# A two-layer hybrid decoder step on one core: feed-forwards that multiply the unnormed sum, low-rank products inside the r and k products, and the first scan unit prepared inside v

## The reference

```python
for i in range(DEPTH):                       # DEPTH = 2
    h = attention(x) if i == 0 else rwkv7_time_mix(x)
    x = layer_norm(ALPHA * x + h, ln_g[i, 0], ln_b[i, 0])
    gu = x @ w_gu[i]
    ffn = (silu(gu[..., :D_FF]) * gu[..., D_FF:]) @ w_down[i]
    x = layer_norm(ALPHA * x + ffn, ln_g[i, 1], ln_b[i, 1])
# rwkv7_time_mix: xr, xw, xk, xv, xa, xg = (x + xx * mix[c] for c in range(6)), xx = previous token - x
# r, k, v = xr @ w_r, xk @ w_k, xv @ w_v
# w = f(tanh(xw @ w1) @ w2), a = sigmoid(a0 + (xa @ a1) @ a2), g = sigmoid(xg @ g1) @ g2
# then a delta-rule scan over the tokens, a group norm, a gate by g and an output product
```

## Time and profile before

| | us |
|---|---|
| median of 3 runs | 1932.48 (1930.57 to 1932.52) |
| the profiled execution | 1942.81 |
| its span | 1941.0 |
| TensorE busy | 1706.0 |
| VectorE, ScalarE, GpSimd busy | 651.9, 687.3, 587.1 |

### The profile page before, as it was taken

The page is one execution under the profiler, slowest core; times in us unless marked ns, Lnnn a source line. Parts: engine busy times, 40 slices in busy tenths (PEclk is TensorE's granted clock), DMA queues, the critical chain, the costliest instruction groups (busy, mean ns, idle before and its releaser), DMA issues.

```text
span 1941.0 us, 46539 instructions
## 1 busy us (share of the span) xinstructions
PE 1706.0 (88%) x20338; PEld 1552.7 (80%) x20338; DVE 651.9 (34%) x897; ACT 687.3 (35%) x1110; POOL 587.1 (30%) x322
## 2 busy tenths in 40 slices
PE   4987969999989967898958888888797999998995
PEld 4975959999989967696647766666496999998995
DVE  2145562222223344404153444443165222222224
ACT  3146253333322122322254455443225333321113
POOL 2324423333333421232142222220142333333430
PEclk8998989999999986999978999999597999999998
DMA  8410222222223213321100001000221222222221
GB/s 249 88 41 1 76 74 87 86 76 86 83 74 89 74 36 102 103 72 48 35 4 15 15 15 26 16 10 10 93 75 43 77 86 76 86 81 84 74 74 49
DMA packets 236120, 125.88 MB, mean 65 GB/s; under 512 B 49211, under 2 KB 233068, under 8 KB 235828
## 3 DMA queue, kind: packets, MB, share of 16 engines
q1 hardware_dynamic: 230770, 113.53, 20.7%
q10 hardware_dynamic: 5218, 10.36, 1.5%
HBM read 116.33 MB, written 12.64 MB: 66 GB/s over the span
## 4 chain that ended last, share of the span: by engine, by line
PE 49%; issue 34%; POOL 7%; DVE 6%; ACT 3%; POOLq 0%; ACTq 0%; DVEq 0%
PE ps L699 32%; POOL wl L552 7%; PE ps L1013 1%; PE ps L904 1%; PE ps L1023 1%; PE ps L1103 1%; ACT S L1490 1%; DVE mf L2069 1%; PE ps L1093 1%; PE ps L1114 1%; PE ps L790 1%; PE ps L1144 1%; PE ps L937 1%; PE ps L1050 0%; PE ps L992 0%
## 5 line engine op out<-in xcount | busy, mean ns | idle before, releaser
L552 POOL TENSOR_TENSOR wl<-raw,wh 128x1024 fp32r<-128x1024 f32 (+1 forms) x172 | 453.5, 2638 | 891.3 <-ACT wh L1371 891.3
L699 PE MATMUL ps<-xh,wh 128*128 128x288 f32 x2112 | 462.4, 301 | 61.8 <-DVE xl L1868 21.0
L1371 ACT CAST wh<-raw 128x1024 fp32r<-128x1024 f32 (+1 forms) x172 | 190.3, 1108 | 829.4 <-PE ps L699 819.9
L699 PE MATMUL ps<-xl,wh 128*128 128x288 f32 x2112 | 457.8, 299 | 0.0
L699 PE MATMUL ps<-xh,wl 128*128 128x288 f32 x2112 | 457.4, 299 | 0.0
L699 PEld LDWEIGHTS ps<-xh,wh 128*128 128x128 f32 x2112 | 345.4, 192 | 73.3 <-issue 41.4
L699 PEld LDWEIGHTS ps<-xl,wh 128*128 128x128 f32 x2112 | 346.1, 192 | 0.0
L699 PEld LDWEIGHTS ps<-xh,wl 128*128 128x128 f32 x2112 | 345.8, 192 | 0.0
L1944 DVE TENSOR_TENSOR lnw<-lnw,ps 128x576 f32<-128x576 f32 x44 | 33.2, 755 | 390.4 <-PE ps L699 373.3
L699 PE MATMUL ps<-hh,wh 128*128 128x288 f32 x704 | 153.3, 300 | 11.3 <-DVE hl L1949 11.3
L699 PE MATMUL ps<-hl,wh 128*128 128x288 f32 x704 | 152.5, 299 | 0.0
(11 more groups left out here) (332 smaller groups left out, 2174.6 us busy)
## 6 DMA issues: line engine op xcount, KB each, us to landing
raw<-in_ffn_w_gu SPq DMA_DIRECT2D x88, 512.0 KB, 3.8
raw<-in_ffn_w_down SPq DMA_DIRECT2D x32, 704.0 KB, 4.5
raw<-in_rwkv_w_rkv SPq DMA_DIRECT2D x24, 512.0 KB, 3.6
raw<-in_attn_w_qkv SPq DMA_DIRECT2D x24, 256.0 KB, 3.7
raw<-in_attn_w_o SPq DMA_DIRECT2D x32, 128.0 KB, 2.9
raw<-in_rwkv_w_o SPq DMA_DIRECT2D x8, 512.0 KB, 3.6
spread<-table ACTq DMA_DIRECT2D x1, 3072.0 KB, 14.5
x_kept<-x SPq DMA_DIRECT2D x1, 2304.0 KB, 8.8
```

The source lines that it names most:

```text
L552: nc.gpsimd.tensor_tensor(wl[:, s, 0:ph.kb, :], raw[:, s, 0:ph.kb, :], wh[:, s, 0:ph.kb, :].bitcast(F32), ALU.subtract).then_inc(raw_free, 1)
L699: out = mm(ps[:, 2 * a + b, 0:TH], w[:, s, k, :], o[:, k0 + k, t0:t0 + TH], start=(first and k == 0 and w is wh and o is high), stop=(last ...
L1371: nc.scalar.copy(wh[:, s, 0:ph.kb, :], raw[:, s, 0:ph.kb, :]).then_inc(hi_done, 1)
```

## The change

Four things are changed.

1. **Feed-forwards.** After wo and ro, ScalarE multiplies each finished block of the sum by the norm's weight into the high part (`summed_product`), VectorE subtracts to get the low part (`add_and_pass_on`); no mean is taken off and nothing is scaled. The operand tiles get two more columns in their first half (`WIDE = TH + 2`, 290 of 288): the norm's weight and its bias, so that each up slab also gives the products of weight row and bias row with the weights. TensorE starts the first up slab on these; the first waits for the columns of blocks 0 to 5, and at block 6 for those of 6 and 7. The statistics' products stand after the first up slab. VectorE scales each output from PSUM by the inverse deviation and adds the two columns' parts (mean times the first, plus the second), for the gate before Silu and for the up part before the product: eight VectorE instructions per hidden block where there were two. The normed, ALPHA-scaled x that the residual needs is made in the loop, a block per round. The loops of ScalarE and VectorE over hidden blocks are written out.
2. **Down products** wait for each hidden block on its own.
3. **r, k, v.** The last slab of wo, r, k and ro counts each operand block that it has used (`given_up`), and the next operand's parts may overwrite that block. Decay and rate products stand between the blocks of r's slabs 2 to 5 (both for the same block, one to each column half), the gate products between the blocks of k's first slab, the shift rows' transposes before r's slab 6.
4. **Slot 0 of the scan** is taken out of the loop and done during v: TensorE's two small products before slab 4 and key sums before slab 6, ScalarE's steps after slabs 3, 5 and 7, GpSimd's between its splits; to have room, `hats` and the first `bt` use other tiles. SP loads the first states when v's operand is complete. The gate's second weights are loaded by ScalarE after v's last read-out; GpSimd's clears of the scan's tiles move with it.

The core of the diff:

```diff
 def slab(..., op=None, between=None, release=None, hidden=None, columns=None):       # TensorE
     for k in range(kb):
         if op is not None:
             pe.wait_ge(op_ready, KB * OP[op] + k + 1)
+        if columns is not None and k in (0, KB - 2):
+            pe.wait_ge(ev("ln_cols"), columns + (1 if k == 0 else 2))
+        if hidden is not None:
+            pe.wait_ge(hid_lo, hidden + k0 + k + 1)
         for w, o in ((wh, high), (wh, low_), (wl, high)):
             for b, t0 in halves:
-                out = mm(ps[:, 2 * a + b, 0:TH], w[:, s, k, :], o[:, k0 + k, t0:t0 + TH],
+                wide = high is sum_h
+                n = WIDE if wide and b == 0 else TH
+                out = mm(ps[:, 2 * a + b, 0:n], w[:, s, k, :],
+                         o[:, k, b, 0:n] if wide else o[:, k0 + k, t0:t0 + TH],
...
+        elif release is not None:
+            out.then_inc(release, 1)
+        if between is not None:
+            between(k)
...
-                pe.wait_ge(hid_lo, FB * (i_ffn + 1))
...
-            norm(0, PH["wo"])
             ffn(0)
...
+            def lora_wa(k):
+                if k == 0:
+                    pe.wait_ge(ev("lora_w_in"), 16 * 6)
+                pe.wait_ge(ev("mf"), 2 * k + 2)
+                for b, t0 in halves:
+                    for w, part, own in ((w1s, top, 0), (a1s, low, 1)):
+                        out = mm(ps[part, 4 + b, 0:TH], w[:, k, :], mf[:, own, t0:t0 + TH], start=(k == 0), stop=(k == KB - 1))
+                out.then_inc(ev("mf_used"), 1)
...
+            mixed_product("r", before={6: shift_rows}, between={m: lora_wa_in(m) for m in range(2, 6)}, release=ev("given_up"))
+            mixed_product("k", between={0: lora_g}, release=ev("given_up"))
+            mixed_product("v", before={4: lambda: lora2(0), 6: lambda: kk_sum(0)})
...
+            def summed_product(name, i_ln):                                          # ScalarE
...
+                def high(j):
+                    act.wait_ge(ev("given_up"), GIVEN[name] + min(j + 2, KB - 1))
+                    A(sum_h[:, j, :, 0:TH], x[:, j, :].rearrange("p (h n) -> p h n", h=2), ACT.Identity, scale=col(R_LNG + i_ln, j)
+                      ).then_inc(op_hi, 1)
...
+                high_ahead(ph, KB - 2, 0, True)
+                squares(KB - 2)
+                for j in range(KB - 2):
+                    high(j)
+                act.wait_ge(ev("given_up"), GIVEN[name] + KB - 1)
+                columns(0, KB - 2)
+                high_ahead(ph, KB - 1, 1, True)
...
+                        g, h = gbuf[:, q, :], hbuf[:, q, :]                            # VectorE, ffn
+                        V.tensor_copy(gate_sc[:, q, :], ps[:, 4 * q, TH:WIDE]).then_inc(ev("ffn_step"), 1)
+                        V.tensor_tensor(halved(g), acc(2 * q), halved(rsd), ALU.mult).then_inc(gate_free, 1)
+                        V.scalar_tensor_tensor(g, centre, gate_sc[:, q, 0:1], g, ALU.mult, ALU.add).then_inc(ev("ffn_step"), 1)
+                        V.tensor_copy(up_sc[:], ps[:, 4 * q + 2, TH:WIDE]).then_inc(ev("ffn_step"), 1)
+                        V.tensor_tensor(halved(h), acc(2 * q + 1), halved(rsd), ALU.mult).then_inc(ev("ffn_step"), 1)
+                        V.scalar_tensor_tensor(h, centre, up_sc[:, 0:1], h, ALU.mult, ALU.add).then_inc(ev("ffn_step"), 1)
+                        dve.wait_ge(ev("gated"), n + 1)
+                        V.scalar_tensor_tensor(h, h, up_sc[:, 1:2], g, ALU.add, ALU.mult).then_inc(up_free, 1)
+                        V.tensor_tensor(hl[:, 2 * i + q, :], h, hh[:, 2 * i + q, :].bitcast(F32), ALU.subtract).then_inc(hid_lo, 1)
...
+                    if i < KB:
+                        normed(i)
...
+                def low_part(j):                                                      # VectorE, add_and_pass_on
+                    dve.wait_ge(op_hi, op + j + 1)
+                    V.scalar_tensor_tensor(sum_l[:, j, :, 0:TH], x[:, j, :].rearrange("p (h n) -> p h n", h=2), col(R_LNG + i_ln, j),
+                                           sum_h[:, j, :, 0:TH].bitcast(F32), ALU.mult, ALU.subtract).then_inc(op_ready, 1)
...
+                added(ph, KB // 2 - 1, 0)
+                summed(ph, i_ln, KB // 2 - 1, 0)
+                for j in range(KB - 2):
+                    low_part(j)
+                columns(0, KB - 2, 1)
+                added(ph, KB // 2 - 1, 1)
+                low_part(KB - 2)
+                low_part(KB - 1)
+                columns(KB - 2, KB, 2)
+                summed(ph, i_ln, KB // 2 - 1, 1)
...
+                        dve.wait_ge(ev("given_up"), (KB - 1) * step + j + 1)           # VectorE, mix
...
-            sp.wait_ge(ev("proj_taken"), 1)
+            sp.wait_ge(op_ready, KB * (OP["v"] + 1))
             sp.wait_ge(ev("x_moved"), 16)
             state_in(0)
             state_in(1)
...
+            split_two(PH["v"], 1)                                                     # GpSimd
+            pool.wait_ge(op_ready, KB * (OP["v"] + 1))
+            nc.gpsimd.memset(cc_s[:], 0.0)
+            nc.gpsimd.memset(cc[:], 0.0).then_inc(ev("wkv_zero"), 1)
+            split_two(PH["v"], 2)
+            split_two(PH["v"], 3)
+            scaled_gate(0)
+            scaled_r(0)
+            scaled_keys(0)
...
-            for s in range(SLOTS):
+            for s in range(1, SLOTS):
```

More of the change, by code:

```diff
@@ L690, in _, with slab @@
             ident = const("ident")
-            def slab(a, s, kb, high, low_, k0, first, last, op=None):
+            def slab(a, s, kb, high, low_, k0, first, last, op=None, between=None, release=None, hidden=None, columns=None):
                 for k in range(kb):
@@ L711, in two_slabs @@
                         pe.wait_ge(acc_free, 2 * i + (ph.m0 + s + 1))
-                        slab(s, s, ph.kb, high, low_, 0, True, True, op)
+                        slab(s, s, ph.kb, high, low_, 0, True, True, op, release=release if s == 1 else None)
                 two_slabs(0, op)
-                with nc.tensor.Fori(1, ph.slabs // 2 - int(before_last is not None)) as i:
+                with nc.tensor.Fori(1, ph.slabs // 2 - int(apart)) as i:
                     two_slabs(i)
@@ L717, in product, with mixed_product @@
                     before_last()
-                    two_slabs(ph.slabs // 2 - 1)
+                if apart:
+                    two_slabs(ph.slabs // 2 - 1, release=release)
+            def mixed_product(name, before={}, between={}, release=None):
+                ph = PH[name]
+                for m in range(ph.slabs):
+                    if m in before:
+                        before[m]()
+                    pe.wait_ge(raw_free, m + ph.n0 + 3)
+                    pe.wait_ge(acc_free, m + ph.m0 + 1)
+                    slab(m % 2, m % 2, ph.kb, xh, xl, 0, True, True, name if m < 2 else None, between.get(m),
+                         release if m == ph.slabs - 1 else None)
             def cache_keys():
@@ L890, in _ @@
             pe.wait_ge(ev("o_taken"), U // 2)
-            product("wo", None)
-            norm(0, PH["wo"])
+            product("wo", None, release=ev("given_up"))
             ffn(0)
-            norm(1, PH["dn0"])
-            def lora_in(step, products):
-                for k in range(KB):
-                    pe.wait_ge(ev("mf"), KB * step + k + 1)
-                    for w, part, bank in products:
-                        for b, t0 in halves:
-                            out = mm(ps[part, bank + b, 0:TH], w(k), mf[:, k % 2, t0:t0 + TH], start=(k == 0), stop=(k == KB - 1))
-                    out.then_inc(ev("mf_used"), 1)
@@ L907, in _ @@
-            product("r", "r")
-            pe.wait_ge(ev("shc"), KB)
-            for j in range(KB):
-                out = nc.tensor.transpose(ps[0:9, 6 + j // 4, (j % 4) * P:(j % 4 + 1) * P], shc[:, j, :], ident)
-            out.then_inc(ev("sh_mm"), 1)
-            pe.wait_ge(ev("lora_w_in"), 16 * 6)
-            lora_in(0, [(lambda k: w1s[:, k, :], top, 4)])
-            product("k", "k")
-            pe.wait_ge(ev("lora_out"), 1)
-            lora_in(1, [(lambda k: a1s[:, k, :], low, 4)])
@@ new lines, in lora_g @@
+            def lora_g(k):
+                if k == 0:
+                    pe.wait_ge(ev("lora_w_in"), 16 * 6)
+                    pe.wait_ge(ev("sh_taken"), 1)
+                    pe.wait_ge(ev("proj_taken"), 1)
+                pe.wait_ge(ev("mf"), 2 * KB + k + 1)
+                for cols, part, bank in ((slice(0, P), slice(0, P), 4), (slice(P, L_GATE), slice(0, L_GATE - P), 6)):
+                    for b, t0 in halves:
+                        out = mm(ps[part, bank + b, 0:TH], g1s[:, k, cols], mf[:, k % 2, t0:t0 + TH], start=(k == 0), stop=(k == KB - 1))
+                out.then_inc(ev("mf_used"), 1)
@@ L1049, in gram_br @@
                     for part in heads2:
-                        out = mm(ps[part, G1, tk(c)], bt[part, i % 2, tk(c)], zr_of(i)[part, c, 1, :], start=True, stop=True)
```

(12 more changed lines are left out.)

380 lines of the change are left out of this document (240 added, 140 removed).

## The result

The changed kernel takes **1855.36 us** (median of 4 runs, 1850.66 to 1856.13) where the kernel before, on the same chip, takes 1932.31: ratio 0.9599, 95% interval 0.9582 to 0.9615, that is 77 us less. The forecast was 1853. The profiled execution took 1850.66 us.

The account below looks back on a forecast made before the run. TensorE was taken as the bound inside the slab loops but not between them. Gains of 23.6 + 16.3 + 33.1 + 6.1 = 79.1 us off the 1932.48 us median gave 1853 us, range 1836 to 1885.

Parts of the forecast that it names:

- Feed-forward start: Hand-over from attention output to up product: excess falls from 23.6 to 11.8 us, gaining 11.8 each, twice 23.6.
- the columns: Up product: two more columns on 576 slow the slabs by 0.35% of 281.6 us, 1.0 us each.
- the late gated block: Feed-forward start: the first gated block runs late on ScalarE, delaying the next cast behind its Silu, estimated 1.0 us.
- Down start: First down slab: waiting per hidden block removes the whole 8.1 us, wait and low clock, twice 16.3.
- r, k and v: End of r to the scan: low-rank products and waits fall from 72.8 to 39.7 us, gaining 33.1.
- From k to v: Hand-over from k to v: mixing is not fully covered and costs 4.5 us, ends 0 and 11.
- Scan slot: First scan slot: the 6.13 us for scaled keys are over before v ends, gaining 6.1, ends 0 and 12.
- Changes of tiling mode: Sixteen insertions between slab products: 32 mode changes drain TensorE, estimated 4 us, giving 1857; the rows show no such gap.
- 1: Low-rank pairs on the two column halves don't overlap: 8.3 us more, 1862 us; chance 0.14.
- 2: VectorE still holds the feed-forward hand-over, with no gain there: 1877 us; chance 0.11.
- 3: VectorE becomes the up loop's pace, each two-operand SBUF step held by GpSimd: 158 us more, 2011 us; chance 0.05.
- 4: Waits only change their names, each new first wait ending when the old one did: about 1932 us; chance 0.02.

Follow-up runs that it names:

- the kernel with the late sums: Changed kernel with VectorE's sums and squares of the last block but one moved behind all low parts and columns: 1856.05 us, ratio 0.9582.
- columns_first: Changed kernel with those sums and squares moved late and VectorE's column operation put before the last two of six low parts: 1845.36 us, ratio 0.9514.

## Why the prediction was right, point by point

- **Feed-forward start** (11.8 of excess each): measured 294.1 - 281.6 = 12.5. The wait was 4.85 and 4.76 (5.0), and the path was the one counted: squares held by a split, then six low parts, one held by the next split. But the count gave the squares too much: without them the wait was still 3.96, since the second split's end sets it. The clock cost 2.1 (the first slab takes 9.1 us, and 7.0 at full clock; forecast 2.5), the statistics 2.1 (2.3), the slab itself 0.5. Two terms were mis-sized and in part cancel: the columns cost 44 x 0.067 = 2.9 and not 1.0, so that the casts lie at 6.467, outside the forecast's sign of 6.40 to 6.45; and the late gated block cost nothing visible and not 1.0.
- **Down start** (8.1 each): shown by two runs, 8.19 and the 24 us that came back. The stages gained 11.7 and 12.4, since the slabs run at 8.58; these 3.5 us each no step of the prediction had. It had seen that the pace moves by 2.5% for reasons no row names, but used it only as a bound of the columns.
- **r, k and v** (39.7 left of 72.8): 30.5 gained, 33.1 forecast. The pairs cost 8 x (9.6 - 6.32)/2 = 13.1 with their waits (11.3 forecast). The gate products make k's first slab 25.7 us (792.74 to 818.47), 19.4 over a plain one (18.1): the products took what was forecast, and 1.36 is a wait for k's operand, which the prediction had hidden below TensorE. From k to v 6.1 (4.5, and "under 6" as its sign): 3.5 of gaps (0.53, 0.53 and 2.42 us), the rest at a clock of 0.70 behind them, which the prediction did not count. The key sums took 1.0 and not 2.05.
- **Scan slot**: 5.7 (6.1). The wait for GpSimd's scaled keys is 1.69 us (L676) where it was 6.13, so it is not over before v ends; beside it the granted clock of the slot rose from 0.77 to 0.96.
- **Changes of tiling mode**: two timelines of the changed kernel show eight float32 records between slab products, 128 columns wide (the statistics) and with the last four 32 wide (a gate block). The first row is the block, the second the slab's second pair of products behind it:

```profile
269.72 2.10 PE L813 MATMUL ps<-lnw,cst 128*128 128x288 f32 x8
...
271.93 0.43 PE L733 MATMUL ps<-xl_all,wh 128*128 128x290 f32 x2
```

```profile
793.54 2.22 PE L972 MATMUL ps<-mf,lnw 128*128 128x288 f32 x8
...
796.06 0.43 PE L733 MATMUL ps<-xl_all,wh 128*128 128x288 f32 x2
```

From row to row are 2.21 us without a change of width and 2.52 with it. The pairs on one column half, 64 wide, take 2.46 (742.74 to 745.20) and start 0.08 us later behind the slab. That is 0.3 us per insertion and some 5 us for sixteen. The Trainium skill (TensorEngine Tiling (Array Packing), Key Properties) has a drain at a change of tiling mode, and the trace agrees in size with the forecast's estimate of 4 us. That these 0.3 us are a drain no run shows by itself. The prediction was wrong that its rows show no such gap: a gate block's 2.26 us hold it, as eight records of one width take 1.94 (2.21 less the 0.27 of one pair of slab products). So only the share of the decay and rate pairs was missing, which is of the size of the 1.8 us by which they exceed their forecast.

- **Rivals**: 1 is refuted and priced (5.3). 2 is refuted in size: VectorE does hold the hand-over, for 4.8 us and not for the whole gain. 3 is refuted here, with at least 3.6 us of slack per block. 4 is refuted by the waits above.
- **A reading and the total**: of the 21.0 us that the earlier trace rows give for L1868, 3.7 stand at the kernel's first product and not at a feed-forward; no term used them. The stages that the forecast names gained 82.6 us in the profiles where it has 79.1: 7.8 more in the down products, 1.3 less at the feed-forward starts, 2.6 less in r, k and v, 0.4 less in the scan slot. The medians differ by 77 on one chip and by 80.7 on another. So the paths were right, but that the total came within 2 us is in part luck: errors of opposite sign, beside a scan that varies by some us.

## What to carry over

Price a hand-over as the excess over the pace of the loop behind it, clock included, and then ask which operation of the slowest chain stands beside GpSimd's next split; in the kernel with the late sums an operation of 0.16 us held the whole product, and with it two places further forward the kernel was 7.5 us faster than the changed one. An engine with slack in a loop can take work until its own chain, waits included, reaches the loop's pace, and the loss beyond that is steep (nothing for four additions, 136 us for eight). A pace that was measured in one place is not a constant: check it in the changed kernel before a term of a few us is explained.

## What the runs showed of the hardware that was not expected

- **The pace has steps.** Slabs with the same instructions took 6.24, 6.32, 6.40 or 6.61 us (130.0, 131.7, 133.3 or 137.8 ns for a product of 288 columns), each constant to a hundredth or two through a product, but for one or two slabs. It can differ between executions of one kernel: the read-out product of columns_first ran at 6.24 in one profile and at 6.40 in the other, its attention output at 6.61 and 6.32. Down slabs stood at 8.58 (130.0 ns) behind an up loop with the two columns and no wait, at 8.80 behind a wait or behind an up loop at 6.40. What chooses the step is open.
- **Two column halves overlap in both orders that were run.** Two products on one half and then two on the other took as long, 1.20 us, as the alternating order, 1.19; all four on one half took 2.15.
- **GpSimd holds VectorE by the operation, not by the share.** An operation with two SBUF operands that begins during a split is held until the split ends, however small it is (0.16 to 2.32 us); the squares above begin at 251.22 and end at 253.93, 0.6 us after their split. One that has begun 0.2 us before the split is not held: in the changed kernel that of 280.64 takes its 0.82 us although a split begins at 280.85. Those of VectorE's scaling with an operand in PSUM keep their 747 ns in every run, though few of them begin during a split. The Trainium skill (GPSIMD Engine Reference, Key points) names the contention with instructions of two SBUF inputs, and the trace agrees. With two splits per block it is at most two holds, so more operations don't mean more holds.
